# The last expert's down product in two halves of the model's width, in a two-layer MoE trunk

## What is computed

```python
h = h + mix
h = h + hierarchical_moe(rmsnorm(h, norm_ffn[layer]), ...)   # top-2 of 8 experts in the best of 4 groups
...
def expert_block(args):
    xb, e = args
    hb = jax.nn.silu(xb @ w_gate[e]) * (xb @ w_up[e])
    return hb @ w_down[e]
...
return rmsnorm(h, final_norm)
```

## Time and profile before

| what | value |
|---|---|
| median of 3 runs | 1251.96 us (1250.61 to 1252.7) |
| profiled execution: device time | 1253.68 us |
| profiled execution: span | 1251.9 us |
| PE busy | 1037.2 us (83%) |
| DVE busy | 479.5 us (38%) |
| ACT busy | 237.4 us (19%) |
| read from HBM | 460.43 MB, 369 GB/s over the span |
| mean granted TensorE clock | 0.904 of full |

### The profile page before, as it was taken

The page is one execution under the profiler, slowest core; times in us unless marked ns, Lnnn a source line. Parts: engine busy times, 40 slices in busy tenths (PEclk is TensorE's granted clock), DMA queues, the critical chain, the costliest instruction groups (busy, mean ns, idle before and its releaser), DMA issues.

```text
span 1251.9 us, 22215 instructions
## 1 busy us (share of the span) xinstructions
PE 1037.2 (83%) x9493; PEld 703.1 (56%) x9493; DVE 479.5 (38%) x1218; ACT 237.4 (19%) x533; POOL 4.2 (0%) x26
## 2 busy tenths in 40 slices
PE   9999999777767485889999999999977675858576
PEld 7888655443334242448888888866544342425243
DVE  2351643432222222336755556464343222222223
ACT  2330211111111111113433334121111111111111
POOL 0000000000000000000000000000000000000000
PEclk9999999878778787999999999999888888879789
DMA  9939799999999999993555553989999999999997
GB/s 381 425 154 386 266 432 430 432 434 431 433 434 428 431 436 431 433 405 138 219 218 219 219 218 152 375 333 431 431 434 431 430 436 432 428 434 435 431 432 300
DMA packets 33240, 462.53 MB, mean 369 GB/s; under 512 B 3696, under 2 KB 3728, under 8 KB 9104
## 3 DMA queue, kind: packets, MB, share of 16 engines
q1 hardware_dynamic: 33120, 461.50, 88.1%
q10 hardware_dynamic: 48, 0.03, 0.0%
HBM read 460.43 MB, written 1.08 MB: 369 GB/s over the span
## 4 chain that ended last, share of the span: by engine, by line
PE 53%; DMA 43%; ACT 1%; DVE 1%; issue 1%; SPq 1%; POOLq 0%; POOL 0%; DVEq 0%; ACTq 0%
DMA front<-in_expert_w_in 36%; PE pa L1489 10%; PE pa L1771 9%; PE pb L1489 8%; PE wa L1771 5%; DMA w_dn<-in_expert_w_down 5%; PE acc L1520 4%; PE wb L1803 3%; PE acc L1631 2%; PE acc L1813 1%; DMA front<-in_e_qk 1%; PE pb L1727 1%; ACT arena L583 1%; PE wa L2065 1%; PE pb L1737 1%
## 5 line engine op out<-in xcount | busy, mean ns | idle before, releaser
L1771 PE MATMUL pa<-front,arena 128*32 128x256 f32 x1792 | 128.8, 451 | 75.9 <-DMA front<-in_expert_w_in 75.9
L1246 DVE TENSOR_SCALAR later<-later 128x128 f32<-128x128 f32 x64 | 14.4, 225 | 412.6 <-ACT later L583 412.6
L1771 PE MATMUL wa<-front,arena 128*32 128x256 f32 x1232 | 100.2, 493 | 86.9 <-DMA front<-in_expert_w_in 83.4
L1771 PEld LDWEIGHTS pa<-front,arena 128*32 128x32 f32 x1792 | 64.0, 129 | 143.1 <-DMA front<-in_expert_w_in 88.2
L1771 PEld LDWEIGHTS wa<-front,arena 128*32 128x32 f32 x1232 | 47.6, 140 | 142.5 <-DMA front<-in_expert_w_in 93.7
L583 ACT ACTIVATE arena<-wb 32x256 f32<-32x256 f32 (+1 forms) x232 | 86.9, 375 | 104.4 <-PE wb L1803 96.1
L1803 PE MATMUL wb<-w_dn,later 128*32 128x256 f32 x1472 | 88.3, 380 | 1.8 <-DMA w_dn<-in_expert_w_down 1.8
L1489 PE MATMUL pa<-hnT,w_x 128*128 128x256 f32 x384 | 85.1, 380 | 0.0
L1489 PEld LDWEIGHTS pa<-hnT,w_x 128*128 128x128 f32 x384 | 72.6, 190 | 9.8 <-issue 0.3
L1771 PE MATMUL wa<-w_x,arena 128*32 128x256 f32 x896 | 64.4, 452 | 16.3 <-DMA w_x<-in_expert_w_in 16.3
L1489 PE MATMUL pb<-hnT,w_x 128*128 128x256 f32 x336 | 74.5, 380 | 0.0
(11 more groups left out here) (332 smaller groups left out, 1235.2 us busy)
## 6 DMA issues: line engine op xcount, KB each, us to landing
front<-in_expert_w_in SPq DMA_DIRECT2D x40, 4096.0 KB, 25.2
w_dn<-in_expert_w_down SPq DMA_DIRECT2D x46, 2048.0 KB, 25.8
w_x<-in_expert_w_in SPq DMA_DIRECT2D x14, 4096.0 KB, 35.8
arena<-in_expert_w_down SPq DMA_DIRECT2D x14, 2048.0 KB, 26.5
front<-in_expert_w_in SPq DMA_DIRECT2D x6, 2048.0 KB, 9.3
front<-in_expert_w_in SPq DMA_DIRECT2D x12, 1024.0 KB, 7.4
w_x<-in_o_bc SPq DMA_DIRECT2D x8, 1024.0 KB, 6.0
w_x<-in_o_x SPq DMA_DIRECT2D x8, 1024.0 KB, 4.9
```

The lines of the kernel that those rows point to most:

```text
L1246: link(v.tensor_scalar(eg, eg, 1.0, None, ALU.add))
L1771: ins = mm(gu[32 * j:32 * j + 32, :, :], xb[:, k, c0:c0 + CAP], w[k][:, :, P * j:P * j + P], start=(k == 0), stop=(k == KC - 1))
```

## The change

It touches expert 31 of each layer and what follows it.

- **Loads.** The down page of expert 31 comes in five pieces in place of three: model columns 0 to 511 of row blocks 0 and 1, the same columns of blocks 2 and 3 (0.5 MB each), then columns 512 to 1023 of blocks 0 and 1 (0.5 MB), of block 2 and of block 3 (0.25 MB each). A contiguous run in HBM is 2 KB long for all of them.
- **Products.** `last_down(l, n)` does the products c = 2n and 2n+1 of `down`, `last_combine(l, n)` the matmuls c = 2n and 2n+1 of `combine`. ACT copies each half alone. PE's order is: down half 0, wait for its copy, combine half 0, down half 1, (layer 0: the first set of dt and square sums,) wait for the copy, combine half 1.
- **Layer 0.** DVE's `raw` and ACT's squares of banks 0 and 1 begin after combine half 0, those of banks 2 and 3 after combine half 1. ACT's order is bank 1, 0, (copy of half 1), 3, 2. The four `warm` matmuls behind expert 31 are gone.
- **Layer 1.** ACT squares model half 0 of both token halves first, with the copy of half 1 between the two, then model half 1. DVE's two `weighted` and `mean_square` wait accordingly.

```diff
-                    sp_.dma_start(dn3_parts[0], rows[:, 0:2, :]).then_inc(S["dn_in3"], 16)
-                    sp_.dma_start(dn3_parts[1][:, 0:1, :], rows[:, 2:3, :]).then_inc(S["dn_in3b"], 16)
-                    sp_.dma_start(dn3_parts[1][:, 1:2, :], rows[:, 3:4, :]).then_inc(S["wv_in0b"], 16)
+                    for n in range(2):
+                        c = slice(D // 2 * n, D // 2 * n + D // 2)
+                        sp_.dma_start(dn3_parts[0][:, :, c], rows[:, 0:2, c]).then_inc(S[("dn_in3", "wv_in0b")[n]], 16)
+                        if n == 0:
+                            sp_.dma_start(dn3_parts[1][:, :, c], rows[:, 2:4, c]).then_inc(S["dn_in3b"], 16)
+                            continue
+                        sp_.dma_start(dn3_parts[1][:, 0:1, c], rows[:, 2:3, c]).then_inc(S["wv_in0c"], 16)
+                        sp_.dma_start(dn3_parts[1][:, 1:2, c], rows[:, 3:4, c]).then_inc(S["wv_in0d"], 16)
...
+            def last_first_half(l):
+                act.wait_ge(S["dn_half"], l + 1)
+                af(y_halves[0], Y_halves[0], ACT.Copy).then_inc(S["y_half"], 1)
+
+            def last_second_half(l):
+                act.wait_ge(S["dn_done"], NE * l + NE)
+                af(y_halves[1], Y_halves[1], ACT.Copy).then_inc(S["y_copied"], 1)
...
-            act.wait_ge(S["comb_part"], NE + 4)
-            for b in (2, 3, 0, 1):
-                if b < 2:
+            act.wait_ge(S["comb_half"], 1)
+            for b in SQUARED:
+                if b == 3:
+                    last_second_half(0)
+                    act.wait_ge(S["comb_part"], NE + 4)
+                if b % 2 == 0:
                     act.wait_ge(S["raw_in"], b + 1)
...
-            act.wait_ge(S["comb_part"], 2 * NE + 4)
-            for t, i in norm_parts():
-                if t and i == 0:
-                    act.wait_ge(S["y_ready"], 1)
+            act.wait_ge(S["comb_half"], 2)
+            for t, i in ((0, 0), (1, 0), (0, 1), (1, 1)):
+                if (t, i) == (1, 0):
+                    last_second_half(1)
+                if (t, i) == (0, 1):
+                    act.wait_ge(S["comb_part"], 2 * NE + 4)
...
-                dve.wait_ge(S["comb_part"], NE * (l + 1) + 4)
                 if l == 0:
+                    dve.wait_ge(S["comb_half"], 1)
                     for c in range(4):
-                        if c > 1:
-                            dve.wait_ge(S["sq_part"], 5 + c - 1)
+                        if c == 2:
+                            dve.wait_ge(S["comb_part"], NE + 4)
+                        if c % 2:
+                            dve.wait_ge(S["sq_part"], 5 + c)
...
             dve.wait_ge(S["fnorm_in"], 16)
-            dve.wait_ge(S["sum_sq"], 1)
+            dve.wait_ge(S["sum_sq"], 2)
             weighted(0)
             mean_square(0)
-            dve.wait_ge(S["sum_sq"], 3)
             weighted(1)
...
+            def last_down(l, n):
+                for j in range(4):
+                    if j == 0 and n:
+                        pe.wait_ge(S["wv_in0b"], 16 * l + 32)
+                    if j == 2:
+                        if n:
+                            pe.wait_ge(S["wv_in0c"], 16 * l + 32)
+                        else:
+                            pe.wait_ge(S["dn_in3b"], 16 * uses(DSLOT, 3, NE) * (l + 1))
+                    if j == 3 and n:
+                        pe.wait_ge(S["wv_in0d"], 16 * l + 32)
+                    for c in (2 * n, 2 * n + 1):
+                        ins = mm((Y_ps, Y_last)[n][32 * c:32 * c + 32, :], o_hT[:, 32 * j:32 * j + 32],
+                                 dn_rows[3][j][:, 256 * c:256 * c + 256], start=(j == 0), stop=(j == 3))
+                return ins
+
+            def last_combine(l, n):
+                g4, y = G4[QUAD - 1], yq[:, QUAD - 1, :]
+                for i in range(2):
+                    for c in (2 * n, 2 * n + 1):
+                        r, half = slice(32 * c, 32 * c + 32), slice(P * i, P * i + P)
+                        a, m = (g4[r, half], y[r, :]) if l else (y[r, half], g4[r, :])
+                        ins = mm(acc[:, c, 256 * i:256 * i + 256], a, m,
+                                 start=False, stop=False, skip_group_check=True, tile_position=(32 * c, 0))
+                return ins
+
+            def dt_and_squares(n):
+                b = SQUARED[n]
+                pe.wait_ge(S["raw_in"], n + 1)
+                for k in (2 * n, 2 * n + 1):
+                    mm(wb[0:HEADS, 0:SEQ], wdt[:, k, :], raw[:, k, :], start=(k == 0), stop=(k == KC - 1))
+                pe.wait_ge(S["sq_part"], 5 + n + 1)
+                for k in (2 * b, 2 * b + 1):
+                    ins = mm(wb[HEADS:HEADS + 1, 0:SEQ], esum[:, NG + NE:], hsq[:, k, :],
+                             start=(k == 2 * SQUARED[0]), stop=(k == 2 * SQUARED[3] + 1))
+                return ins
+
+            def last_expert(l):
+                pe.wait_ge(S["dn_in3"], 16 * uses(DSLOT, 3, NE) * (l + 1))
+                pe.wait_ge(S["ht_done"], NE * l + NE)
+                pe.wait_ge(S["g4_done"], NE * l + NE)
+                last_down(l, 0).then_inc(S["dn_half"], 1)
+                pe.wait_ge(S["y_half"], l + 1)
+                last_combine(l, 0).then_inc(S["comb_half"], 1)
+                last_down(l, 1).then_inc(S["dn_done"], 1)
+                if l == 0:
+                    pe.wait_ge(S["par_in"], 16)
+                    dt_and_squares(0)
+                pe.wait_ge(S["y_copied"], NE * l + NE)
+                last_combine(l, 1).then_inc(S["comb_part"], 1)
...
-                down_of(l, NE - 1)
-                sum_alone(l, NE - 1)
-                if l == 0:
-                    warm(4)
+                last_expert(l)
```

More of the change, by code:

```diff
@@ L44 @@
 ALONE = NE - QUAD
+SQUARED = (1, 0, 3, 2)
 NORMS = 5
@@ L106 @@
 gu_half prep_sel quad_sel b_done g4_done gath_done xs_done gu_done gexp h_done ht_done dn_done y_copied comb_part
+dn_half y_half comb_half
 order_done w_vec w_act w_b w_gu w_dn w_done
@@ L259, in trunk_program @@
         last0 = arena[:, CHUNK:2 * CHUNK]
+        y_halves = [yq[0:64, QUAD - 1, :], yq[64:P, QUAD - 1, :]]
         sel = take(P, rows=NE)
@@ L322, in trunk_program @@
         Y_ps, Y_last = wb[:, 256:512], pb[:, 256:512]
+        Y_halves = [wb[0:64, 256:512], pb[64:P, 256:512]]
         GU = [b[:, 0:256].rearrange("p (g n) -> p g n", g=2) for b in (wa, pa)]
@@ L726, in output_alone @@
                     act.wait_ge(S["comb_part"], ALONE + (NE * l + 4))
-                af(yq[:, e - ALONE, :], Y_last if e == NE - 1 else Y_ps, ACT.Copy).then_inc(S["y_copied"], 1)
+                af(yq[:, e - ALONE, :], Y_ps, ACT.Copy).then_inc(S["y_copied"], 1)
+            def last_first_half(l):
[4 more added lines that the diff above has]
+                af(y_halves[1], Y_halves[1], ACT.Copy).then_inc(S["y_copied"], 1)
             def moe(l):
@@ L762, in moe @@
                                 overflow(k)
-                output_alone(l, NE - 1)
+                last_first_half(l)
             moe(0)
@@ L1296, in moe @@
                         ins.then_inc(S["raw_in"], 1)
-                    for n, c in enumerate((2, 3, 0, 1)):
+                    for n, c in enumerate(SQUARED):
                         dve.wait_ge(S["sq_part"], 5 + n + 1)
@@ L1313, in _ @@
             for k in range(KC):
-                dve.wait_ge(S["h_part"], 5 + (k // 2 + 2) % 4 + 1)
+                dve.wait_ge(S["h_part"], 5 + SQUARED.index(k // 2) + 1)
                 v.scalar_tensor_tensor(hnT[:, k, :], resT[:, k, :], norm_w[:, 1, k:k + 1], wb[:, SEQ:],
@@ L1450, in mean_square @@
             def mean_square(t):
-                dve.wait_ge(S["sum_sq"], 2 * t + 1)
+                dve.wait_ge(S["sum_sq"], t + 1)
                 link(v.tensor_scalar(sums[:, t, 2:3], sums[:, t, 0:1], 1.0 / D, EPS, ALU.mult, ALU.add))
-                dve.wait_ge(S["sum_sq"], 2 * t + 2)
+                dve.wait_ge(S["sum_sq"], t + 3)
                 v.scalar_tensor_tensor(st[:, 5, t:t + 1], sums[:, t, 1:2], 1.0 / D, sums[:, t, 2:3], ALU.mult, ALU.add
@@ L1792, in first_gate_up, with down @@
                 ins.then_inc(S["gu_done"], 1)
-            def down(ht, rows, turn=0, y=Y_ps, half_in=None, last_in=None):
+            def down(ht, rows, turn=0, y=Y_ps, half_in=None):
                 for j in range(4):
-                    if last_in is not None and j == 3:
-                        pe.wait_ge(S["wv_in0b"], last_in)
                     if half_in is not None and j == 2:
@@ L1872, in down_of @@
                 pe.wait_ge(S["ht_done"], NE * l + e + 1)
[L1873 to L1876, removed]
                 if NE * l + e:
@@ L2000, in raw_bc @@
                 return ins
[L2002 to L2010, removed]
+            for n in (1, 2, 3):
+                ins = dt_and_squares(n)
             ins.then_inc(S["ss_done"], 1)
```

## The result

The change makes the kernel slower. The median is 1255.28 us (1254.64 to 1256.12, 8 runs) against 1252.2 us for the kernel before in its 8 runs; the ratio is 1.0027 with a 95% interval of 1.0019 to 1.0036. On 1252 us that is 3.4 us, from 2.4 to 4.5 (the two medians lie 3.1 us apart). The prediction was 3.8 us and 1255.8 us.

What follows compares the result with a forecast made beforehand. The kernel was taken as alternating between weight stream and PE, with the expert stages' two ends deciding; losses of 1.4 us (layer 0) and 2.4 us (layer 1) made 3.8, on 1251.96 giving 1255.8 us, range 1253.6 to 1257.6.

Steps and rivals of the forecast that it cites:

- What bounds the two ends: Behind expert 30's last down page, each layer's end hangs on PE, ACT or DVE; data wait about 0.1 us a cycle.
- The cost of a half product: Expert 31: a half down keeps 8 steps of about 0.215 us, costing 1.9 us like the whole; half combine 1.1 us.
- The rival that half a product costs half: Expert 31's half products save 2.6 us a layer, giving 1250.6 us, not slower; chance 0.10.
- The data: Expert 31's down page arrives at about 400 GB/s, so neither half waits; 1.0 us kept for the range.
- Layer 0: Behind layer 0's experts: combine ends 3.38 us later, early work gives some back, loss 1.4 us.
- the case in which sums and products keep their order: Layer 0's first sums run behind half 1, 1.1 us more, loss 2.5 us; chance 0.08 shared with late data.
- Layer 1: Behind layer 1's experts: combine ends 3.40 us later, first store 2.5, last store's scale 2.2; loss taken as 2.4 us.
- Does the loss of layer 0 reach the end: The forecast counted layer 0's 1.4 us in full, as the chain runs through the mixer into layer 1's weight stream.
- the rival: Layer 1's weight stream swallows layer 0's loss, giving 1254.4 us; chance 0.07.
- The clock: Rival: the granted clock falls in layer 0 without the warm matmuls, up to 6 us more, up to 1262 us; chance 0.04.

Runs made afterwards that it cites:

- e3: The kernel before with only the change's five loads, whole product and order kept; ratio 0.9998 (0.999 to 1.0007), -0.3 us.
- e4: The change with the three loads of the kernel before, so half 0 waits for the whole page; ratio 1.0032 to the kernel before, +4.0 us.
- e1: The kernel before with the change in layer 0 alone; ratio 1.0011 (1.0003 to 1.002), +1.4 us.
- e2: The kernel before with the change in layer 1 alone; ratio 1.0018 (1.0009 to 1.0027), +2.3 us.
- e5: The change with both half down products issued before PE waits for the first half's copy; ratio 1.0027 to the kernel before, +3.4 us.
- e8: The change's product order with before's loads, halves of 128 columns of all four banks, nothing behind begun early; ratio 1.0023 to the kernel before, +2.9 us.
- e7: The kernel before with 20 in place of 4 warm matmuls behind layer 0's experts; ratio 1.0031 (1.0019 to 1.0043), +3.9 us.
- e6: The kernel before with 128-column halves of expert 31's down product, both per row block as it lands, then both half combines; ratio 1.0002, +0.3 us.
- e9: e6 with the last norm's weights loaded without waiting for pieces of the last down page; ratio 0.9999 to the kernel before, -0.1 us.
- e10: e5 with half 1's copy ahead of the squares and its combine ahead of layer 0's first sums; ratio 1.0007 to the kernel before, +0.9 us.

## Why the prediction was right

**What bounds the two ends.** Right, with one correction. Everything behind expert 30's product hangs on PE, ACT and DVE, and the wait for expert 31's data was small: e3, which changes the loads alone, changes nothing that can be measured, and e4, which keeps the old loads, loses as much as the change. But the stage isn't always left at the landing of expert 30's page. In layer 0 of e1, e2, e4 and e5 PE's gate and up product of expert 31 took 5.3 us and not 3.66, at a granted clock of 0.72 to 0.83 from 545 to 551 us (1.00 in before), and PE went on to expert 30's down product without a wait for DMA. The distances compared here begin behind that point, so they stand, but it is one reason why positions differ.

**The cost of a half product.** Right, and this term carried the forecast. A half took 1.92 us in both layers (1.9 predicted), a half combine 1.13 to 1.16 us (1.1), and combine of half 1 ended 6.99 and 7.02 us behind the start (7.1 in both). e8 tests the reason: with 8 steps as before, but half as wide, the half product fell to 1.08 us, though it has twice the matmuls. The rival that half a product costs half is refuted.

**The data.** Right. Half 0 never waited; PE's rows show no DMA wait, and e3 puts the rate at some 410 GB/s (400 taken).

**Layer 0.** The loss was 1.46 us in the trace (1.4 predicted) and 1.4 us timed (e1). The first set of sums ran beside half 1, as taken: L1858 begins at 558.51 while half 1's last matmuls begin from 558.69 on. So matmuls queued behind half 1's last ones began ahead of them, and the case in which sums and products keep their order and layer 0 loses 2.5 us did not occur. Part of the fit is luck: the two cycles took 6.99 us where 7.11 was summed, and the way from combine to the copy of the row sums took 2.97 us where 2.81 was summed (each pair of `raw` took 0.83 us and not 0.80, and the last set of sums began 1.88 us behind combine, not 1.72). The two misses nearly cancel.

**Layer 1.** 2.25 us in the trace and 2.3 timed (e2), against 2.4. The 2.4 was a choice between 2.5 by the first store and 2.2 by the last; the end of the span moved by 2.3. The part mis-sized is the way from combine to the first store: 2.62 us were summed and 2.44 measured (1247.41 to 1249.85). DVE had done the first of the two small instructions of the mean while it waited, so only the second stood between the sum and POOL (0.35 us from 1248.11 to 1248.46, where 0.49 was taken).

**Does the loss of layer 0 reach the end.** The profiled execution alone would have pointed to the rival, as both kernels start expert 30's product of layer 1 at the same time. e1 (1.4 us, interval above 0) and e7 (3.3 us put in, 3.9 measured) refute it. That the loss does not show in the positions of that one trace I put down to the drift between executions; where between 564 and 924 us it was made up there, was not looked for.

**The clock.** No sign of it: in the change's trace the granted clock was 1.00, full, from 554 to 564 us and from 1240 to 1247.4 us, and the steps took 0.215 us.

The measured 3.4 us lies 0.3 below the 3.7 of the trace, well inside its interval. What stays open: for e8 the trace explains 2.0 of 2.9 us, and why two products back to back share some steps and not all (2.8 us in e5) was not tried.

## What to carry to other kernels

Before a product is cut in two, look at what runs side by side in it: if four small matmuls share a step, a cut that halves their number leaves the steps as they are, and here the time halved only when each was made narrower as well. Even so no version with halves was measurably faster than the whole product (e6, e8, e9, e10). A half that is done early is worth only what can start on it, and a copy or a matmul of the other half that stands behind that early work in its engine's queue gives the gain back (e5 against e10). When a stage is compared between two executions, compare distances from an event just ahead of the edit: the positions drifted by 2.7 us here, nearly the size of the effect. When a stage gets shorter, look for the load that was just in time for it (e6 against e9).

## What the runs showed of the hardware that was not expected

Two products in different array columns, issued back to back with no wait between them that held PE, overlapped only in part: 32 records in 2.8 us, where 1.9 us is the whole and 3.6 us two in a row (e5). The half combines did the same, 1.68 us for both (e10). In e5 the overlap began 0.9 us, four steps, behind the first matmul. And in the change matmuls of another sort, queued behind a product, began while four records of that product were still to start (558.51 against 558.69 and 558.91).
